# Two activation parts as one 512-column operand in a two-term float32r product

## The reference

```
for layer in 0, 1:
    xn = rms_norm(x, norm_mix[layer])
    x = x + (even_mixer if layer == 0 else odd_mixer)(xn, ...)     # odd: q, k, v of 3 groups x 16 heads, rope, dilated attention, @ w_o
    x = x + square(relu(rms_norm(x, norm_mlp[layer]) @ w1)) @ w2   # 1024 -> 4096 -> 1024
x = rms_norm(x, norm_final)
h = rms_norm_2(x, g) @ w_in        # 1024 -> 2*512 + 3*512 + 512 + 3*1024
x = x + (sum over 3 branches of sigmoid(gate) * (branch @ w_branch)) @ w_out
f = rms_norm_2(x, g2)
x = x + (gelu(conv(f @ w_gate)) * (f @ w_up)) @ w_down             # 1024 -> 3072 -> 1024
```

## Time and profile before

| | |
|---|---|
| median of 3 runs | 1346.8 us (1343.91 to 1348.12) |
| the profiled execution's own time | 1344.69 us |
| its span | 1342.9 us |
| granted PE clock, mean share of full speed | 0.979 |
| PE busy | 1266.7 us (94%) |
| DVE busy | 836.9 us (62%) |
| ACT busy | 621.2 us (46%) |
| POOL busy | 272.3 us (20%) |
| memory read | 206.31 MB |

### The profile page before, as it was taken

How to read it: one execution, slowest core, us unless ns; L and a number is a source line. 1 busy time by engine, 2 the same in 40 slices (tenths; PEclk the granted TensorE clock), 3 DMA queues, 4 the chain that set the end, 5 groups by cost and what they waited for, 6 DMA issues and landing times.

```text
span 1342.9 us, 23879 instructions
## 1 busy us (share of the span) xinstructions
PE 1266.7 (94%) x10309; PEld 1221.3 (91%) x10309; DVE 836.9 (62%) x1107; ACT 621.2 (46%) x760; POOL 272.3 (20%) x119
## 2 busy tenths in 40 slices
PE   4999999999999999998789999998989898999997
PEld 3987789999999999998689999998989888999997
DVE  4657656655565566666756655484777676555653
ACT  4456445544444455444355544345456445444431
POOL 4400050000012112110130000275311365433100
PEclk9998989999999999999989999998999998999998
DMA  8731345555566654554236555553534353555550
GB/s 207 218 126 63 120 131 170 181 185 188 189 197 220 188 180 151 181 160 163 64 95 188 189 181 178 178 167 122 194 129 154 118 165 126 189 187 177 179 181 32
DMA packets 198214, 215.19 MB, mean 160 GB/s; under 512 B 9763, under 2 KB 186222, under 8 KB 198110
## 3 DMA queue, kind: packets, MB, share of 16 engines
q1 hardware_dynamic: 192510, 205.08, 47.4%
q10 hardware_dynamic: 4896, 7.08, 1.8%
q0 software_dynamic: 704, 1.51, 0.7%
HBM read 206.31 MB, written 1.05 MB: 154 GB/s over the span
## 4 chain that ended last, share of the span: by engine, by line
PE 74%; DVE 10%; ACT 7%; issue 5%; DMA 2%; POOL 1%; ACTq 0%; SPq 0%; DVEq 0%; POOLq 0%
PE ps L487 67%; ACT whi L895 3%; PE ps L577 2%; PE ps L612 1%; DVE XL L1303 1%; PE ps L585 1%; DMA raw<-in_ev_w_in_dram 1%; DVE BIG L1712 1%; ACT SN L957 1%; POOL wlo L1909 1%; DVE XT L1393 1%; DVE XT L1386 1%; DVE BIG L1792 1%; DVE SN L1337 1%; PE ps L511 1%
## 5 line engine op out<-in xcount | busy, mean ns | idle before, releaser
L487 PE MATMUL ps<-XH,whi 128*128 128x256 f32 x1720 | 494.8, 289 | 15.6 <-ACT XH L927 9.3
L1269 DVE TENSOR_TENSOR wlo<-raw,whi 128x2048 fp32r<-128x2048 f32 x152 | 353.7, 2329 | 234.1 <-ACT whi L895 233.9
L487 PE MATMUL ps<-XL,whi 128*128 128x256 f32 x1720 | 490.3, 286 | 2.4 <-DVE XL L1303 1.6
L487 PE MATMUL ps<-XH,wlo 128*128 128x256 f32 x1720 | 487.9, 285 | 0.0
L895 ACT ACTIVATE whi<-raw 128x2048 fp32r<-128x2048 f32 x190 | 361.3, 1903 | 190.4 <-PE ps L487 156.3
L487 PEld LDWEIGHTS ps<-XH,whi 128*128 128x128 f32 x1720 | 333.7, 195 | 21.8 <-ACT XH L927 11.5
L487 PEld LDWEIGHTS ps<-XL,whi 128*128 128x128 f32 x1720 | 333.1, 194 | 4.4 <-DVE XL L1303 2.9
L487 PEld LDWEIGHTS ps<-XH,wlo 128*128 128x128 f32 x1720 | 333.1, 194 | 0.2
L1909 POOL TENSOR_TENSOR wlo<-raw,whi 128x2048 fp32r<-128x2048 f32 x38 | 176.3, 4644 | 484.4 <-ACT whi L895 484.4
L487 PE MATMUL ps<-HH,whi 128*128 128x256 f32 x832 | 229.5, 283 | 0.0
L487 PE MATMUL ps<-HL,whi 128*128 128x256 f32 x832 | 229.3, 283 | 0.0
(11 more groups left out here) (217 smaller groups left out, 1506.8 us busy)
## 6 DMA issues: line engine op xcount, KB each, us to landing
raw<-in_mlp_w_dram SPq DMA_DIRECT2D x64, 1024.0 KB, 5.4
raw<-in_od_w_in_dram SPq DMA_DIRECT2D x36, 1024.0 KB, 5.4
raw<-in_w_in_dram SPq DMA_DIRECT2D x24, 1024.0 KB, 5.2
raw<-in_w_ffn_gate_dram SPq DMA_DIRECT2D x12, 1024.0 KB, 5.2
raw<-in_w_ffn_up_dram SPq DMA_DIRECT2D x12, 1024.0 KB, 5.1
raw<-in_w_ffn_down_dram SPq DMA_DIRECT2D x12, 1024.0 KB, 5.1
raw<-in_ev_w_in_dram SPq DMA_DIRECT2D x7, 1024.0 KB, 12.8
TB<-TA ACTq DMA_DIRECT2D x96, 64.0 KB, 4.2
```

The source lines that it names most:

```text
L487: m = pe.matmul(to, l[c][a], r[c][b], start=first and k == 0, stop=last and k == 3 * n - 1)
L1269: dve.tensor_tensor(wlo_of(n), raw_of(n), f32(whi_of(n)), ALU.subtract).then_inc(*tell(s_wlo, ("wlo", n)))
```

## The change

High and low part of each activation are laid side by side in one tile (`XHL`, `OHL`, `HHL`: 2 x 256 columns for each chunk). The high weights now meet both parts in one matmul of 512 columns, and the low weights meet the high part in one of 256 columns, which is added into the upper half of the same bank. So the lower half holds whi by XH, the upper half whi by XL plus wlo by XH, and whoever reads a product has to add the two halves. A product of 256 features takes two banks instead of one. `tokens` is left as it is.

The banks are now split in pairs: outside the attention steps 0-1, 2-3, 4-5, 6-7 are given out in turn; during them the pairs 0-1 and 2-3 go to products and banks 4 to 7 singly to scores, transposes and values.

```diff
+            def product(to, w, x, event=None, first=True, last=True, late=False):
+                n = len(w)
+                order = [(c, a) for c in range(n) for a in range(2)]
...
+                    if a == 0:
+                        m = pe.matmul(to, w[c][0], x[c][0], start=first and k == 0, stop=False)
+                    else:
+                        m = pe.matmul(to[:, S:2 * S], w[c][1], x[c][1], start=False, stop=last and k == 2 * n - 1)
...
+            def join(dst, use, *events):
+                once.wait_ge(*at(("product", *use)))
+                i = bank_of.get(use, 0)
+                dve.tensor_reduce(dst, PS[:, i:i + 2, :].rearrange("p m (a t) -> p m t a", a=2), AX.X, ALU.add).then_inc(
+                    *tell(s_dve_out, ("taken", *use), ("joined", *use), *events))
+                once.wait_ge(*at(("joined", *use)))
```

`join` is a reduction of 128x1024 in PSUM to 128x512 in SBUF. It stands ahead of the former operation in `scaled`, `first_queries`, `rotary_key`, `down`, `branch`, `ffn_conv`, `ffn_high` and `odd_slab`, and that operation now reads SBUF. The residual additions are done twice, once for each half:

```diff
-                dve.tensor_tensor(o, o, pair(b[:, :]), ALU.add).then_inc(*tell(s_dve_out, ("taken", "onto", n, j)))
+                dve.tensor_tensor(o, o, PS[:, i:i + 2, 0:S], ALU.add).then_inc(*tell(s_dve, ("half added", n, j)))
+                once.wait_ge(*at(("half added", n, j)))
+                dve.tensor_tensor(o, o, PS[:, i:i + 2, S:2 * S], ALU.add).then_inc(
+                    *tell(s_dve_out, ("taken", "onto", n, j), ("added", n, j)))
```

`onto_natural` has four additions of 256 columns instead of two. In the MLP, ACT copies the upper halves (no ReLU), DVE adds the lower halves, and max and square are one operation:

```diff
-                    once.wait_ge(*at(("relu", layer, j)))
-                    dve.tensor_tensor(z, a, a, ALU.mult).then_inc(*tell(s_dve, ("h", layer, j)))
+                    once.wait_ge(*at(("low sum", layer, j)))
+                    dve.tensor_tensor(pair(a), PS[:, i:i + 2, 0:S], pair(a), ALU.add).then_inc(
+                        *tell(s_dve_out, ("taken", *use), ("summed", layer, j)))
+                    once.wait_ge(*at(("summed", layer, j)))
+                    dve.scalar_tensor_tensor(out=z, in0=a, scalar=0.0, in1=a, op0=ALU.max, op1=ALU.mult).then_inc(
+                        *tell(s_dve, ("h", layer, j)))
```

In the odd layer ACT's copy goes away; `join` writes `TA`, and ACT's four transfers wait for it:

```diff
-                act.activation(TA[k][:, :], b[:, :], ACT.Copy, scale=1.0).then_inc(*tell(s_act_out, ("copied", n)))
-                once.wait_ge(*at(("copied", n)))
+                once.wait_ge(*at(("halves", swaps[0])))
...
-                b = take(("slab", n), [("copied", n)])
-                dve.tensor_tensor(pair(QKV[hb % 3][i]), pair(b[:, :]), twice(RP[:, 0:S]), ALU.mult).then_inc(
-                    *tell(s_dve_out, ("taken", "slab", n)))
+                join(pair(TA[k % 2][:, :]), ("slab", n), ("halves", k))
+                dve.tensor_tensor(pair(QKV[hb % 3][i]), pair(TA[k % 2][:, :]), twice(RP[:, 0:S]), ALU.mult).then_inc(
+                    *tell(s_dve, ("made", n)))
```

More of the change, by code:

```diff
@@ L465, in tensor, with emptied @@
             once = Once(pe)
[L466 to L471, removed]
+            used, taken = [None] * 8, {"pair": 0, "single": 0}
+            pairs = [0, 2, 4, 6]
+            def emptied(i, use):
                 if used[i] is not None:
@@ L474, in bank, with banks @@
                 used[i] = use
-                bank_of[use] = i
[L476 to L481, removed]
-                if late:
[L483 to L487, removed]
+            def banks(use):
+                i = pairs[taken["pair"] % len(pairs)]
+                taken["pair"] += 1
+                emptied(i, use)
+                emptied(i + 1, use)
+                bank_of[use] = i
+                return PS[:, i, :], PS[:, i + 1, :]
+            def bank(use):
+                i = 4 + taken["single"] % 4
+                taken["single"] += 1
+                emptied(i, use)
+                bank_of[use] = i
+                return PS[:, i, :]
+            def product(to, w, x, event=None, first=True, last=True, late=False):
+                n = len(w)
+                order = [(c, a) for c in range(n) for a in range(2)]
+                if late:
+                    order = [(c, a) for a in range(2) for c in range(n)]
+                for k, (c, a) in enumerate(order):
+                    once.wait_ge(*at(w[c][2 + a]))
+                    once.wait_ge(*at(x[c][3]))
+                    once.wait_ge(*at(x[c][4]))
+                    if a == 0:
+                        m = pe.matmul(to, w[c][0], x[c][0], start=first and k == 0, stop=False)
+                    else:
+                        m = pe.matmul(to[:, S:2 * S], w[c][1], x[c][1], start=False, stop=last and k == 2 * n - 1)
                 if event is not None:
@@ L647, in mlp @@
                         sums(norm, slot)
-                down(layer, W2[layer], h_ready(layer, 32))
-            b = bank(("mixgain",))
+                for j in range(4):
+                    down(layer, W2[layer], h_ready(layer, 32), j)
+            b = banks(("mixgain",))[0]
             once.wait_ge(*at("mixrows"))
@@ L1035, in scalar @@
                     root("nq", 1)
-                    square("nk", 1, 0, CK, ("taken", "slab", 4), ("norm", "nk"), after="cq")
+                    square("nk", 1, 0, CK, ("made", 4), ("norm", "nk"), after="cq")
                 if s == 2:
@@ L1531, in vector @@
                     ahead(3)
-                    b = take(("slab", 3))
-                    dve.tensor_tensor(CQ, pair(b[:, :]), twice(r0), ALU.mult).then_inc(*tell(s_dve_out, ("taken", "slab", 3)))
+                    scaled(3, CQ)
                 if s == 1:
@@ L1679, in vector @@
             mlp(1, "n3", 0, follow_both, decay)
-            def scaled(n, dst, by=1.0):
-                b = take(("slab", n), ["both"])
-                dve.scalar_tensor_tensor(out=dst, in0=pair(b[:, :]), scalar=by, in1=twice(R), op0=ALU.mult, op1=ALU.mult).then_inc(
-                    *tell(s_dve_out, ("taken", "slab", n)))
             def factors():
```

314 lines of the change are left out of this document (169 added, 145 removed).

## The result

The changed kernel takes 1501.22 us (median of four, 1498.9 to 1504.85), beside 1347.46 for the kernel before on the same chip: ratio 1.1148, 95% interval 1.1113 to 1.1183 (for every run below, the ratio to the kernel before and this interval stand in brackets). It is slower, as forecast, but by 154 us and not by 71. The profiled execution took 1498.9 us, its span is 1497.1.

What follows compares the result with a forecast made beforehand. It took closed rounds of DVE and ACT waiting for each other, close beside PE's pace, as deciding. Its terms summed to +70.8 us on the profiled 1344.7, giving 1415 us, range 1365 to 1450.

Steps and rivals of the forecast that it cites:

- even layer: Even layer: doubled additions of two projections, four more at its end and joins of first slabs and memory: +11 us.
- two MLPs: Both MLPs: first half unchanged, second half gains 5.9 us less 1.6 at the end of a block: -8.6 us together.
- odd attention, first ten slabs: Odd layer's attention: a round rises from 6.9 to 8.9 us, transfers and exponentials waiting behind the join: +28 us.
- odd projection: Odd layer's projection: additions double in 6 steps and at the end, 17.6 us less 1.5 of PE: +16 us.
- second stack and gates/branches: 24 joins for gates and branches go into a round already the bound, +24 us; the second stack's 12 slabs, +7.
- feed-forward to the end: Feed-forward and last product: DVE keeps 1 us spare per pair of slabs, PE keeps its gain: -11.6 us.
- PE's pace: Matmul stream: a chunk takes 335 instead of 358 ns, 23 ns less; 63.5 us in all if PE set the pace everywhere.
- the store of the MLPs: MLPs' first half: about 6 us of work held ahead absorbs part of the 11.7 us deficit over 16 slabs.
- the ring in which VectorE waits for ScalarE: Closed round of DVE and ACT waiting for each other sets the pace: 6.1 us a slab in the MLP's first half.
- The rival that PE sets the pace everywhere: Whole kernel: work in store outlasts the DVE-ACT rounds, so the change is faster, 1295 us; chance 0.10.
- The rival "PE gains nothing": Slabs where a gain was counted: PE gains nothing per matmul, 0.37 us missing each, +25, 1440 us; chance 0.06.
- the 7 of the rival: Odd attention: the transfers stay out of its round, so +7 us instead of +28, 1394 us; chance 0.15.

Runs made afterwards that it cites:

- banks_only: Changed kernel with three 256-column matmuls a chunk into the lower half and the earlier kernel's single readers, so only bank layout and buffers are new: 1370.57 us (1.0168).
- one_bank_even: banks_only, but in the even layer's attention a product lies in the two halves of one bank, with four turns instead of two pairs: 1349.9 us (1.0009).
- onto_lower: Changed kernel with a single addition of the lower halves in every projection (even, odd, last layer), low parts left out there: 1474.57 us (1.0937).
- mlp_lower: Changed kernel with the MLPs' first products read as before, lower halves only and relu on ScalarE: 1488.28 us (1.1020).
- wide_lower_read: Changed kernel with wide matmul and bank pairs kept, but readers take the lower half only, without joins or added operations: 1353.15 us (1.0034).

## Why the prediction was right in direction and half in size

By its own terms, against the starts of the same instructions in the two traces:

```
term                              predicted   measured
even layer                              +11      +31.0
two MLPs                               -8.6      +12.4
odd attention, first ten slabs          +28      +43.8
odd projection                          +16      +21.4
second stack and gates/branches         +31      +33.9
out2                                     +5       +5.6
feed-forward to the end               -11.6       +6.1
sum                                   +70.8     +154.2
```

(The second MLP is taken from the end of the projection to the last low part of the activations for the second stack, +103.9 to +108.7 us. The 83 us between the sums are, by the steps below and rounded: PE's pace 18, the even layer 20, the store of the MLPs 13, the feed-forward's multiplication 8, the odd attention 16, the projection 5, the rest 3.)

**Right.** A join of 1.22 us; the ring in which VectorE waits for ScalarE as the thing that decides; 6.19 us in the MLP (predicted 6.1) and 8.2 among the gates (8.3); the transfers behind the join as the odd layer's largest item; the doubled additions in the projection. The rival that PE sets the pace everywhere was wrong by 200 us.

**The first step that failed is PE's pace.** The prediction took 12.6 ns over the columns for a loss that a matmul longer than 119 ns does not have, from the float32 matmuls of the earlier trace rows. The traces show about 13 ns for each of these matmuls, 256 or 512 columns, and some 5 for their alternation: 7 ns a chunk saved, not 23. The prediction had named 12.6 ns a chunk as the other end of its bounds; the measured 7 lies even below that, by the alternation. It is 17 us over the kernel instead of 63; in the slabs where the sum counted a gain, 0.11 us a slab instead of 0.37 make 18 us (68 x 0.26). The rival "PE gains nothing", with 25 us, was the nearer one.

**The second is the even layer: a cost that was not in the sum.** The prediction gave four banks fewer in store a share only in out2. In fact a product that takes two banks leaves two turns beside the attention, and the additions free them late: 26.5 us by banks_only, of which one_bank_even gets 20 back. The joins and additions there cost 7.6 in the one trace (6 to 13 with its scatter), near the predicted 11.

**The third is the store of the MLP.** A deficit of 0.7 us a slab was to be absorbed by 6 us in store. None was: 92.9 us from the first to the sixteenth low part is 15 x 6.2, the ring from the start, where before it was 84.0. The argument for the steady pace was right (6.1 predicted, 6.19 measured); the 6 us of store were a reckoning that no row showed.

**The fourth is the feed-forward.** The prediction left 1 us of DVE's slack there. But `join` into SBUF turns a multiplication with one PSUM operand into one with two SBUF operands, and in the changed kernel it starts while GpSimd works on a low part: 3.84 to 4.39 us in ten of twelve, where it took 0.68. The round is 12.3 us a pair, DVE-bound. The Trainium skill (SBUF — State Buffer, Who interferes with whom) states this: a VectorE instruction with two SBUF inputs contends with a GpSimd instruction that reads SBUF. The runs agree (3.84 to 4.39 us beside GpSimd, 0.69 without), and the prediction should have priced each operand that the change moves from PSUM to SBUF. Its bound for a join was looked for in the join, and the cost was in the instruction behind it.

**Mis-sized:** the odd attention. The place of the transfers was priced at 21 us (28 against 7) and is 27, and their lateness, which was thought to lie within "some 9 for waits", another 16 (from the waits, as said). The sum also gave nine rounds 6.5 us, below the 7.4 that it had itself read for PE's slab and attention: up to 8 us too few. Without both, the joins cost 4 us in the attention itself (234.1 against 230.1), near the 7 of the rival. The projection cost 21 instead of 16; that the clock fell to 0.76 there goes with PE's pauses (58.68 us busy of 88.70), and was not tested apart; onto_lower had half the additions and a higher clock at once, so it does not part the two.

Left open: why mlp_lower gives 21 us in its profiled execution and 13 by the medians, and what the 8 or so joins of the second stack cost; no run took them out. The parts that were taken out one at a time (43, 27, 30, 13 and 8 us) come to 121 of the 148 us that separate the changed kernel from wide_lower_read.

## What to carry to other kernels

A merged matmul that leaves the columns as they are saves only the overhead of one instruction (13 ns at most here, and 7 with the alternating lengths), while what must undo the merge is paid on another engine for each result: price that side by its rings first. When a change moves an operand from PSUM to SBUF, or gives a result two banks, look up who else works in SBUF then and how many results were in store. And of a transfer moved behind a new wait, ask separately what stands behind it in its queue and who waits for its data: both had a price here.

## What had not been expected of the hardware

- float32r matmuls in a stream with a weight load each start 119 ns apart at 256 columns and 227 at 512, 12.6 and 13.7 ns over their columns at 2.4 GHz; the float32 matmuls of the earlier trace rows had 2 or 3 ns over theirs. Alternating 512 and 256 took 351 ns where the two paces add to 346.
- A multiplication of 512 elements a partition with both operands in SBUF took up to 4.39 us beside a GpSimd subtraction of 4.6, and 0.69 without it. In the ten cases in the feed-forward it ended 0.55 us after the subtraction, as if it had waited for it. A multiplication with one PSUM operand (L1839 of the kernel before) took 0.69 us in all ten cases inside a GpSimd subtraction. The joins (`TENSOR_REDUCE`, one PSUM operand) were never stretched: 1.21 to 1.23 us throughout.
- Two SBUF operands are not needed for it: a `TENSOR_SCALAR` with a single one (L1779 of the changed kernel) took 4.83 us beside a GpSimd subtraction and 0.42 alone.
